# A two-layer attention and convolution network on one core: attention over two pairs of blocks at a time, x loaded first and not spilled, three banks in the first stage, the weights' high parts ahead of the root

## The reference

```
hn = rmsnorm(h, norm_g[i])
u = hn @ w_in[i]                      # 2048 -> 5632
a_val, a_glu, a_z, q, k, v, b_z = split(u)
ya = silu(layernorm(conv31(a_val * sigmoid(a_glu)))) * silu(a_z)
yb = window_attention(q, k, v, bias, sink) * silu(b_z)
h = h + concat(ya, yb) @ w_out[i]
e = rmsnorm(p[i] @ w_pe[i], pe_g[i])
h = h + e * sigmoid(h @ w_pg[i])
```

## Time and profile before

| what | us |
|---|---|
| median of three runs (2655.51 to 2656.34) | 2655.87 |
| the profiled execution, its own time | 2656.61 |
| its span in the trace | 2654.8 |
| PE busy | 2621.5 |
| PEld busy | 2123.7 |
| DVE busy | 1492.2 |
| POOL busy | 1103.1 |
| ACT busy | 964.4 |

### The profile page before, as it was taken

One profiled execution on the slowest core, in us unless ns is written; L12 is line 12 of the kernel. 1 busy time (PEld: TensorE's weight loads), 2 busy tenths in 40 slices (PEclk: granted clock), 3 DMA queues, 4 the chain that ended last, 5 costly groups with the idle time before them and its releaser, 6 DMA issues.

```text
span 2654.8 us, 34449 instructions
## 1 busy us (share of the span) xinstructions
PE 2621.5 (99%) x12104; PEld 2123.7 (80%) x12104; DVE 1492.2 (56%) x2388; ACT 964.4 (36%) x1524; POOL 1103.1 (42%) x456
## 2 busy tenths in 40 slices
PE   7999999999999999999999999999999999999999
PEld 5888877778888888888777788888888888888887
DVE  7788777550043267887775500443675787522743
ACT  5222244442153242222444421543421565422521
POOL 3444432234444444444322344444444454444442
PEclk9999999999999999999999999999999999999999
DMA  8222222233323332222222232333333232322222
GB/s 304 96 95 98 93 86 82 76 114 116 98 100 113 133 126 95 95 95 94 84 83 76 111 119 96 102 111 126 106 108 126 89 103 96 140 97 95 96 95 103
DMA packets 77667, 283.51 MB, mean 107 GB/s; under 512 B 8256, under 2 KB 14912, under 8 KB 73600
## 3 DMA queue, kind: packets, MB, share of 16 engines
q1 hardware_dynamic: 77568, 282.20, 31.4%
HBM read 265.36 MB, written 19.96 MB: 107 GB/s over the span
## 4 chain that ended last, share of the span: by engine, by line
PE 93%; DVE 4%; issue 2%; ACT 1%; POOL 0%; POOLq 0%; DVEq 0%; ACTq 0%
PE acc L1301 20%; PE acc L1303 20%; PE acc L1302 20%; PE sc L1301 4%; PE sc L1303 4%; PE sc L1302 4%; PE acc L1325 3%; PE acc L1327 3%; PE acc L1329 3%; PE sc L1325 3%; PE sc L1329 3%; PE sc L1327 3%; PE sc L1434 1%; PE att L1459 1%; PE tr L1448 1%
## 5 line engine op out<-in xcount | busy, mean ns | idle before, releaser
L404 POOL TENSOR_TENSOR WL<-raw,WH 128x1024 fp32r<-128x1024 f32 x452 | 1102.9, 2445 | 1527.9 <-ACT WH L416 1527.7
L1301 PE MATMUL acc<-XH,WH 128*128 128x512 f32 x2432 | 958.5, 394 | 4.7 <-DVE XL L763 3.5
L1303 PE MATMUL acc<-XH,WL 128*128 128x512 f32 x2432 | 948.7, 390 | 0.0
L1302 PE MATMUL acc<-XL,WH 128*128 128x512 f32 x2432 | 948.1, 390 | 0.0
L416 ACT ACTIVATE WH<-raw 128x1024 fp32r<-128x1024 f32 x452 | 474.0, 1056 | 1123.7 <-PE acc L1303 731.9
L1301 PEld LDWEIGHTS acc<-XH,WH 128*128 128x128 f32 x2432 | 457.8, 188 | 104.2 <-issue 5.6
L1303 PEld LDWEIGHTS acc<-XH,WL 128*128 128x128 f32 x2432 | 457.4, 188 | 96.6
L1302 PEld LDWEIGHTS acc<-XL,WH 128*128 128x128 f32 x2432 | 458.0, 188 | 94.1 <-issue 1.5
L763 DVE SCALAR_TENSOR_TENSOR Y<-tr,lv,Y 128x497 f32 (+7 forms) x240 | 176.6, 736 | 2.9 <-DVE T L842 2.9
L763 DVE SCALAR_TENSOR_TENSOR T<-tr,lv,T 128x498 f32<-128x498 f32 (+6 forms) x224 | 164.8, 736 | 0.0
L1301 PE MATMUL sc<-XH,WH 128*128 128x512 f32 x384 | 150.6, 392 | 0.0
(11 more groups left out here) (221 smaller groups left out, 2850.4 us busy)
## 6 DMA issues: line engine op xcount, KB each, us to landing
raw<-in_w SPq DMA_DIRECT2D x452, 512.0 KB, 3.5
h_spill<-H SPq DMA_DIRECT2D x12, 1024.0 KB, 6.2
H<-h_spill SPq DMA_DIRECT2D x12, 1024.0 KB, 7.3
a<-bias_band SPq DMA_DIRECT2D x16, 384.0 KB, 3.2
H<-in_x SPq DMA_DIRECT2D x4, 1024.0 KB, 9.4
bias_band<-bias_line SPq DMA_DIRECT2D x1, 3072.0 KB, 18.9
out<-H SPq DMA_DIRECT2D x3, 1024.0 KB, 8.2
a<-in_pin SPq DMA_DIRECT2D x3, 512.0 KB, 5.7
```

What stands on the lines that cost most here:

```text
L404: pool.tensor_tensor(WL[:, c], raw[:, c], WH[:, c].bitcast(F), ALU.subtract).then_inc(wl_ready, 1)
L1301: pe.matmul(bank, WH[:, c], xh, start=first, stop=False)
L1302: pe.matmul(bank, WH[:, c], xl, start=False, stop=False)
L1303: return pe.matmul(bank, WL[:, c], xh, start=False, stop=last)
```

## The change

**Start.** x comes in five parts (tiles 0-1, 2-3, and three of four tiles) right after unit 0 and is not spilled; layer 0 reads it back from x itself. The small tables come last. PE begins with three matmuls on a tile of zeros, ACT with a copy of one column. The bias line's matmul stands after tile 0 of the first stage, its addition on DVE at the eighth square; the high part of unit 1 is made before XH 6.

**First stage.** Its tiles go round three banks (TRIO). stat stands after four units in both layers. ACT makes the high parts of units 4 to 7 before the root.

**Attention.** Pairs are taken two at a time (two adjacent query blocks of the same heads), 35 steps: at even steps scores (four banks) and values, at odd steps the transposes of four probability blocks, which share two of the score banks. The values of the two blocks are joined: keys that both see are one matmul on 256 columns. The bias has one place instead of two.

```diff
-Z_STEPS = PAIRS + 4
+TWOS = PAIRS // 2
+Z_STEPS = PAIRS + 3
...
+def two_of(m):
+    first, second = pair_of(2 * m), pair_of(2 * m + 1)
+    both = (second[3], second[3] + 1)
+    lone, half = (first[3], 0) if first[4] == 3 else (second[3] + 2, 1)
+    return both, lone, half
...
+        TRIO = (G[0], G[1], SC[0])
...
+        X_PARTS = ((0, 2), (2, 4), (4, 8), (8, 12), (12, 16))
...
+        S_BANKS = (SC, (VB, N))
+        T_BANKS = (TR, SC)
...
             load(0, 0)
+            load_x(0)
             sp.dma_start(v2[:, :], vec2).then_inc(vec2_in, 16)
-            load_x(0)
+            load_x(1)
+            load_x(2)
+            load(1, 1)
+            load_x(3)
+            load_x(4)
+            load(2, 2)
+            load(3, 3)
             sp.dma_start(ones[0:32, 0:HQ], relb).then_inc(relb_in, 16)
...
             for s in range(RING):
                 sp.wait_ge(wl_ready, s + 1)
                 load(RING + s, s)
-                if s < 2:
-                    for c in (2 * s, 2 * s + 1):
-                        sp.wait_ge(h_in[c], 16)
-                        h_dma(c, True)
...
-                for t in range(2, CT):
-                    sp.wait_ge(scores_taken, ly * (2 * PAIRS) + 2 * NB * (t - 1))
+                for t in range(1, CT):
+                    sp.wait_ge(scores_taken, ly * (2 * PAIRS) + 2 * NB * t)
                     load_bias(t)
...
+            act.wait_ge(tile_out, 1)
+            act.activation(sm[:, 0:1], eps[:, 0:1], ACT.Copy).then_inc(warm, 1)
+            act.wait_ge(raw_in[0], 16)
+            high(0)
...
+                for k in range(4):
+                    prep(u0, k)
                 root(rs[:, :], ly * 4 + 1, 1.0 / D)
...
+                def probs_out(m):
+                    if m:
+                        act.wait_ge(pv_done, ly * TWOS + m)
+                    for q in range(2):
+                        n = 2 * m + q
+                        nk = pair_of(n)[4]
+                        k0 = 0 if nk == 3 or two_of(m)[2] == 1 else 1
+                        for hh in range(2):
+                            act.wait_ge(tr_done, ly * (2 * PAIRS) + (2 * n + hh + 1))
...
-                    if n < PAIRS:
-                        exps(n)
-                    if 2 <= n < PAIRS + 2:
-                        probs_out(n - 2)
+                    if n % 2 == 0 and n // 2 < TWOS:
+                        exps(n // 2)
+                    if n % 2 == 1 and 1 <= n // 2 <= TWOS:
+                        probs_out(n // 2 - 1)
...
                 for n, u in enumerate(UNIT_AT):
-                    if 1 <= n <= PAIRS:
-                        finish(n - 1)
-                    if n < PAIRS:
-                        scores(n)
+                    if n % 2 == 1 and n // 2 < TWOS:
+                        finish(n // 2)
+                    if n % 2 == 0 and n // 2 < TWOS:
+                        scores(n // 2)
...
-                    if 3 <= n < PAIRS + 3:
-                        att_out(n - 3)
+                    if n % 2 == 0 and 2 <= n // 2 < TWOS + 2:
+                        att_out(n // 2 - 2)
...
+            pe.wait_ge(warm, 2)
+            for _ in range(3):
+                pe.matmul(VB[:, :], tl(Y, 0)[:, 0:P], tl(Y, 0), start=True, stop=True)
...
+                def scores(m):
+                    if m:
+                        pe.wait_ge(scores_taken, ly * (2 * PAIRS) + 4 * m)
+                    if m >= 2:
+                        pe.wait_ge(pt_ready, ly * (2 * PAIRS) + 4 * (m - 1))
+                    for q in range(2):
+                        t, b, kt, lo, nk = pair_of(2 * m + q)
+                        for hh in range(2):
...
+                def turn(m):
+                    pe.wait_ge(probs_ready, ly * (2 * PAIRS) + 4 * (m + 1))
...
+                    pe.wait_ge(scores_taken, ly * (2 * PAIRS) + 4 * min(m + 2, TWOS))
...
+                def values(m):
+                    kt = pair_of(2 * m)[2]
+                    both, lone, half = two_of(m)
+                    pe.wait_ge(pt_ready, ly * (2 * PAIRS) + 4 * (m + 1))
+                    k0 = 1 if half == 0 else 0
+                    for kb, k in ((both[0], k0), (lone, 0 if half == 0 else 2), (both[1], k0 + 1)):
+                        cols = slice(half * BLK, (half + 1) * BLK) if kb == lone else slice(0, 2 * BLK)
+                        for hh in range(2):
+                            v0 = VT * S + kb * 2 * P + (2 * kt + hh) * DH
+                            last = pe.matmul(TR[0][hh * DH:(hh + 1) * DH, cols], H[:, v0:v0 + DH],
+                                             turned(m, hh)[:, k, cols],
+                                             start=(kb == both[0]), stop=(kb == both[1]))
                     last.then_inc(pv_done, 1)
...
-                    if n < PAIRS:
-                        scores(n)
-                    if 3 <= n < PAIRS + 3:
-                        values(n - 3)
-                    if 2 <= n < PAIRS + 2:
-                        turn(n - 2)
+                    if n % 2 == 0:
+                        if n // 2 < TWOS:
+                            scores(n // 2)
+                        if 2 <= n // 2 < TWOS + 2:
+                            values(n // 2 - 2)
+                    elif 1 <= n // 2 <= TWOS:
+                        turn(n // 2 - 1)
```

More of the change, by code:

```diff
@@ L197, in build @@
         w_used = sem("w_used")
+        x_in = [sem(f"x_in{c}") for c in range(5)]
+        warm = sem("warm")
         h_in = [sem(f"h_in{c}") for c in range(4)]
@@ L784, in _ @@
                 xlow(t, tl(H, t), t + 1, v2[:, W_NORM + t:W_NORM + t + 1])
-                if t == 3:
+            for t in range(NT):
+                if t == 8:
                     dve.wait_ge(line_mm, 1)
@@ L1387, in _, with a_tile @@
                 x0 = ly * (3 * NT)
-                if ly == 0:
-                    tile(n0, u0, 0, G[0], x0)
-                    pe.wait_ge(tile_out, n0 + 2)
-                    unit(u0 + 2, 2, 0, G[1])
+                def a_tile(n, u, k, x_first=None, first=NT):
+                    if ly or first >= 3:
+                        pe.wait_ge(tile_out, n)
+                    unit(u, 2 * k % RING, 0, TRIO[k % 3], x_first)
+                    unit(u + 1, (2 * k + 1) % RING, 1, TRIO[k % 3], x_first)
+                if ly == 0:
+                    a_tile(n0, u0, 0, x0, 0)
+                    pe.wait_ge(relb_in, 48)
+                    pe.matmul(SC[0][0:HQ, :], ones[0:32, 0:HQ], T[0:32, 0:S], start=True, stop=True).then_inc(line_mm, 1)
+                    a_tile(n0 + 1, u0 + 2, 1, None, 1)
+                    pe.wait_ge(ident_in, 16)
+                    pe.wait_ge(line_ready, 1)
                     pe.wait_ge(ones_ready, 1)
-                    pe.wait_ge(hsum_ready, NT)
-                    stat()
-                    unit(u0 + 3, 3, 1, G[1])
                 else:
@@ L1426, in _ @@
                     last.then_inc(vtr_done, 1)
-                def scores(n):
-                    t, b, kt, lo, nk = pair_of(n)
-                    if n:
-                        pe.wait_ge(scores_taken, ly * (2 * PAIRS) + 2 * n)
-                    for hh in range(2):
-                        r = slice(hh * DH, (hh + 1) * DH)
-                        pe.matmul(SC[hh][:, 0:nk * BLK], tl(H, QT + t)[r, b * BLK:(b + 1) * BLK],
-                                  tl(H, KT + kt)[r, lo * BLK:(lo + nk) * BLK],
-                                  start=True, stop=True).then_inc(scores_done, 1)
@@ L1438, in turn, with scores @@
-                def turn(n):
-                    nk = pair_of(n)[4]
-                    pe.wait_ge(probs_ready, ly * (2 * PAIRS) + (2 * n + 2))
-                    if n == 0:
+                def scores(m):
+                    if m:
+                        pe.wait_ge(scores_taken, ly * (2 * PAIRS) + 4 * m)
+                    if m >= 2:
+                        pe.wait_ge(pt_ready, ly * (2 * PAIRS) + 4 * (m - 1))
+                    for q in range(2):
+                        t, b, kt, lo, nk = pair_of(2 * m + q)
+                        for hh in range(2):
+                            r = slice(hh * DH, (hh + 1) * DH)
+                            pe.matmul(S_BANKS[q][hh][:, 0:nk * BLK], tl(H, QT + t)[r, b * BLK:(b + 1) * BLK],
+                                      tl(H, KT + kt)[r, lo * BLK:(lo + nk) * BLK],
+                                      start=True, stop=True).then_inc(scores_done, 1)
@@ L1451, in values @@
-                def values(n):
-                    _, _, kt, lo, nk = pair_of(n)
-                    pe.wait_ge(pt_ready, ly * (2 * PAIRS) + (2 * n + 2))
-                    if n:
-                        pe.wait_ge(att_ready, ly * PAIRS + n)
-                    for k in range(nk):
-                        for hh in range(2):
-                            v0 = VT * S + (lo + k) * 2 * P + (2 * kt + hh) * DH
-                            last = pe.matmul(VB[hh * DH:(hh + 1) * DH, 0:BLK], H[:, v0:v0 + DH],
```

(11 more changed lines are left out.)

214 lines of the change are left out of this document (108 added, 106 removed).

## The result

| | before | after |
|---|---|---|
| median of the runs | 2655.88 (2655.51 to 2656.59) | 2641.47 (2640.41 to 2641.72) |
| the profiled execution, its own time | 2656.61 | 2640.41 |
| its span | 2654.8 | 2638.6 |

The ratio of the times is 0.9944 (95% interval 0.993 to 0.9959), a gain of 14.4 us by the medians. The forecast was 2640, faster. The spans differ by 16.2 us, the forecast sum was 15.7. That the total agrees does not say that its terms do.

The account below looks back on a forecast made before the run. TensorE, holding 93% of the chain, was taken as the bound. Gains 7.5+0.6+6.6+1.0 = 15.7 us took the profiled 2656.61 to 2640.9, called 2640 for a median; 2633 to 2648 takes in all but A, E and tails.

Parts of the forecast that it names:

- start: First five units: earlier x and sums, with the third bank covering the root chain, gain 7.5 us, bounds 4 and 9.
- layer 1's start: PE's 0.6 us wait for a bank there is covered by unit order: gain 0.6 us (0 to 0.9).
- attention, both layers: Paired scores, joined values and grouped transposes save PE 3.3 us per layer, 6.6 in all; bounds 4 and 11.
- end of attention: Last values fill PE's first XL stall of Y, att_out delays XL: gain 0.5 us per layer, 1.0; bounds -1 and 3.
- output projection's loads: SP's queue: reloading x in the same size and place, and unit loads held behind bias loads, cost 0.
- +2.2: Start: POOL work from the early high parts holds DVE's final addition of the sums, making the sum 2.2 us later.
- the 8.7 us: Start: time from the stat matmul until root, reciprocal and eviction are through and the first bank is free.
- edges 0.18: Attention: 0.18 us added to each even step (2.89 us in all) and each odd step (1.25).
- rival D: Larger gain: 9 us at the start and 10 in attention, giving 2635; chance 0.10.
- Slack 2.0: Attention: copied transposes ready at 12.1, PE comes at 14.1; one POOL hold up to 2.4 uses it up, counted 0.
- the 0.9 let go: Attention: half of the remaining 1.8 us, of 70.8 per layer, in small waits and window edges, assumed to go.
- rival A's mild form: Attention: PE waits on the bank ring after POOL holds, 0.25 us a round over 28 rounds, giving 2647; chance 0.12.

Follow-up runs that it names:

- first profile: The unaltered kernel after the change, in its first profiled execution: 2640.41 us.
- the second: The kernel after the change, unaltered, profiled once more: median 2640.9 us, profiled execution 2641.90.
- the best kernel: Kernel after plus running sums in PSUM, first four output units' loads ahead of the 4 MB, DVE's attention-output copy early and ACT's transpose copies first: 2629.14 us.
- two moves: Kernel after with DVE's attention-output copy right behind the score reductions (alone 2643.44 us) and ACT's transpose copies first at odd steps (alone 2640.14); both: 2636.1.
- three edits: Kernel after plus running sums in PSUM, first four output units' loads ahead of the 4 MB, and DVE's attention-output copy early: 2636.89 us.

## Why the prediction was right, and where it was not

| term | forecast, us | first profile, us |
|---|---|---|
| start | 7.5 | 5.3 (3.7 in the second) |
| layer 1's start | 0.6 | 0.9 |
| attention, both layers | 6.6 | 10.1 |
| end of attention | 1.0 | 1.2 |
| output projection's loads | 0 | -1.3 |
| sum | 15.7 | 16.2 |

The end of attention is what the steps of the table above leave beside the groups. The total was right within 1.5 us of the median, and that is luck: the start gave 2.2 less than forecast and attention 3.5 more.

**Start, up to unit 4: right.** XL 0 begins at 7.9 (said: ready at 8.4), stat at 39.78 (38.7 to 39.4), unit 4 at 40.31 (near 40.0). Within it the last XL came 3.1 us earlier than said, at 22.1 instead of 25.2, because POOL's subtractions came 0.9 later and met two additions instead of two XL. In my sum no running addition was held; two were, for 4.4. The hold of the final addition, "+2.2", was 2.1. That the three holds together decide is shown: with the sums in PSUM the time falls by 6.4. What the final one is worth alone was not run.

**Start, unit 5: wrong.** The failed step is "So stat begins at 38.7 to 39.4 and ends near 40.0, and the third bank lets unit 4 begin at once; units 4 and 5 (10.9 us) cover the 8.7 us". Unit 4 began at once, but the two took 12.9: unit 4 took 7.5 us instead of 5.4. In the best kernel, at the full clock, it takes 5.9 behind stat; the other 1.6 are the stretch of 3.4 us at a granted clock of 0.50. The kernel before had such a stretch too, 39.3 to 42.7, and it cost nothing there: PE was through with its fourth unit 0.49 us before unit 4's low part was ready at 47.51, and without the stretch it would have waited longer. I had counted slow stretches ahead of stat only. The wait that the change removes had been hiding the cost of this one.

**Attention: right in sign, mis-sized.** The term is the price of a group: 66.6 us a layer for the groups was forecast, and 61.8 is what they cost (2 x 1.491 + 14 x 2.724 + 2 x 1.442 + 16 x 1.115). I added "edges 0.18" to each group; beside the columns the transposes show 0.05, and scores and values nothing. That is what the upper bound of 11 named (matmuls in a row hide what each pass showed alone), and rival D, with 10 in attention, had a chance of 0.10. Without its waits the attention would have gained 16.6 us in both layers (70.15 a layer before, measured in the same way, with some 0.9 of waits in it).

**Attention's waits: wrong.** "Slack 2.0: one POOL hold of up to 2.4 ... just uses it up. I count 0." Of the slack I followed one loop, the scores behind the copies; that one shows 0.7 a layer. The other, transposes behind the attention output's copy, I never laid out, and it shows 2.6 a layer. Together 3.3 a layer against the 0.9 let go. Over 28 rounds that is 0.24 us a round, the size that rival A's mild form had (0.25); of it 0.05 is in the loop that A named. The time did not come out at A's 2647 because the groups are so much cheaper.

**Spills and SP's order: one miss.** "The reload comes from x in the same size and place: 0." The place in the program is the same, the place in time isn't: attention brings PE there 5.7 us earlier, and the loads behind the 4 MB don't follow. That costs 1.3 us, shown by moving them; with the attention part alone it was 1.1.

**What should show it.** Attention was to cost PE near 67 us a layer, and cost 65.1. There was to be no wait of the scores for ACT's copies, and there are two, 1.2 us in all.

## What to carry to other kernels

Put a stretch of lower clock into the sum wherever PE has waited just before, even if the trace of before shows the same stretch at no cost: ask what hides it there. For a loop over several engines write down every wait of the bounding engine and the chain behind each, with one hold in it; if an edit removes a wait and the time stays, look for the same microseconds under another name before giving the edit up, since here two moves whose medians alone were 2.0 us slower and 0.8 faster were worth 4.8 together. And when the bounding engine gets earlier, check each load that stands behind a large one in the queue.

## What the runs showed of the hardware

- Two profiles of one program had their stretches at the lower clock in different places and of different length (16.7 to 20.1 and 40.6 to 44.0; 8.6 to 12.0 and 39.3 to 46.2), and the time to unit 5 differed by 1.6 us. Over the profiles of all kernels here the lower level was granted for between 0 and 10.3 us of the first 50. Waits of 1.9 us (layer 1's attention, three edits) and 1.76 us (layer 1's output projection, ScalarE's copies first) had a stretch of 3.4 us behind them in one profile each; waits as long had none in others.
- POOL's subtraction holds even an operation on four columns of VectorE: 2.2 us in 8 of 32 cases, 0.17 when free. It is itself stretched, from 2.4 to 4.31 us, beside VectorE's operations with two inputs in SBUF.
- Four float32 score matmuls of 64 rows in a row cost 1.491 us where two groups of two had cost 1.898; splitting value matmuls of 256 columns into twice 128 costs 0.011 for eight records.
